# Five output banks, slot tables before the last gather evictions, tile-wise transfers, and memory products that wait for banks

## The reference, cut to what matters

```python
# per layer, x is (512, 1024), mem is (256, 1024)
x = x + mixers(rms_norm(x)) @ w_mix_out            # latent attention, pooling, window attention, convolution
kv = rms_norm(mem) @ xa_w_kv                       # (256, 512)
x = x + cross_attention(rms_norm(x) @ w_q, kv) @ w_o
t = rms_norm(x)
g = argmax(t @ w_group); top2 = top_k(softmax((t @ w_expert)[group g]), 2)
for e in range(32):                                # only for tokens that chose e
    y = (silu(t_e @ w_gate[e]) * (t_e @ w_up[e])) @ w_down[e]
    x[tokens of e] += weight * y
```

## Time and profile before

| | |
|---|---|
| Median of 3 runs | 1267.82 us (1262.52 to 1271.57) |
| The profiled execution | 1269.59 us, its span 1267.9 us |
| TensorE busy, mean granted clock | 1190.8 us (94%), 0.966 |
| VectorE / ScalarE / GpSimd busy | 696.0 / 326.3 / 46.4 us |
| Chain that ended last | PE 85%, DVE 7%, issue 2%, ACT 2%, DMA 1% |

### The profile page before, as it was taken

The page is one execution under the profiler, slowest core; times in us unless marked ns, Lnnn a source line. Parts: engine busy times, 40 slices in busy tenths (PEclk is TensorE's granted clock), DMA queues, the critical chain, the costliest instruction groups (busy, mean ns, idle before and its releaser), DMA issues.

```text
span 1267.9 us, 17480 instructions
## 1 busy us (share of the span) xinstructions
PE 1190.8 (94%) x5132; PEld 653.3 (52%) x5132; DVE 696.0 (55%) x1627; ACT 326.3 (26%) x731; POOL 46.4 (4%) x89
## 2 busy tenths in 40 slices
PE   6999999999698999999979999999996899999996
PEld 3754555556593444444457545555565744444443
DVE  3345564467674555555542365545767745555554
ACT  4215231024312222222142152211242222222221
POOL 7000000000006000000000000000000000000000
PEclk9999998999798999999989999989997999999999
DMA  9140023400405999999541300245004089999981
GB/s 284 33 132 1 1 67 123 177 34 1 199 1 179 401 422 422 422 422 422 201 143 32 102 1 1 67 133 199 1 2 199 1 316 404 421 422 422 422 374 67
DMA packets 52549, 243.14 MB, mean 192 GB/s; under 512 B 8320, under 2 KB 18848, under 8 KB 27392
## 3 DMA queue, kind: packets, MB, share of 16 engines
q1 hardware_dynamic: 49344, 240.40, 48.0%
q0 software_dynamic: 2560, 1.89, 0.9%
q10 hardware_dynamic: 576, 0.02, 0.0%
HBM read 240.19 MB, written 2.10 MB: 191 GB/s over the span
## 4 chain that ended last, share of the span: by engine, by line
PE 85%; DVE 7%; issue 2%; ACT 2%; DMA 1%; DVEq 1%; ACTq 1%; SPq 0%
PE ps L2519 18%; PE ps L2124 10%; PE ps L2552 9%; PE ps L2344 8%; PE ps L2116 7%; PE ps L2503 6%; PE ps L2504 4%; PE ps L2094 4%; PE ps L2145 4%; PE ps L2489 2%; PE ps L2392 2%; PE ps L2186 2%; PE ps L2488 2%; DMA X<-in_x 1%; PE ps L2194 1%
## 5 line engine op out<-in xcount | busy, mean ns | idle before, releaser
L2519 PE MATMUL ps<-wgu,xw 128*64 128x512 f32 x1024 | 228.8, 600 | 7.8 <-ACTq L1179 6.7
L1958 DVE TENSOR_TENSOR X<-ps,X 128x512 f32<-128x512 f32 x256 | 156.0, 682 | 10.9 <-issue 9.0
L2124 PE MATMUL ps<-hT,ring 128*128 128x512 f32 x352 | 158.4, 606 | 0.0
L2519 PEld LDWEIGHTS ps<-wgu,xw 128*64 128x64 f32 x1024 | 76.8, 138 | 153.9 <-issue 153.9
L2552 PE MATMUL ps<-wdn,hhT 128*64 128x512 f32 x512 | 120.3, 613 | 2.8 <-ACTq L1197 2.8
L2344 PE MATMUL ps<-ring,yT 128*128 128x512 f32 x256 | 119.5, 616 | 0.4 <-DVE X L1356 0.4
L2503 PE MATMUL ps<-yhi,Wt 128*128 128x512 f32 x256 | 114.1, 446 | 3.7 <-DVEq L1242 3.7
L2124 PEld LDWEIGHTS ps<-hT,ring 128*128 128x128 f32 x352 | 67.4, 196 | 78.2 <-issue 78.2
L2504 PE MATMUL ps<-ylo,Wt 128*128 128x512 f32 x256 | 101.1, 395 | 0.0
L1976 DVE SCALAR_TENSOR_TENSOR ylo<-ps,ws,yhi 128x512 fp32r<-128x512 f32 x64 | 48.1, 751 | 74.1 <-ACTq L1207 74.1
L1965 DVE TENSOR_TENSOR hh<-ps,silu 128x256 f32<-128x256 f32 x32 | 13.6, 425 | 124.6 <-ACTq L1185 124.6
(11 more groups left out here) (367 smaller groups left out, 1505.0 us busy)
## 6 DMA issues: line engine op xcount, KB each, us to landing
wgu<-in_w_gate SPq DMA_DIRECT2D x64, 1024.0 KB, 9.0
wgu<-in_w_up SPq DMA_DIRECT2D x64, 1024.0 KB, 11.1
wdn<-in_w_down SPq DMA_DIRECT2D x64, 1024.0 KB, 10.9
ring<-in_w_in SPq DMA_DIRECT2D x8, 1024.0 KB, 6.6
ring<-in_w_mix_out SPq DMA_DIRECT2D x12, 512.0 KB, 6.0
w_kv<-in_xa_w_kv SPq DMA_DIRECT2D x2, 2048.0 KB, 10.0
ring<-in_w_in SPq DMA_DIRECT2D x2, 2048.0 KB, 17.6
ring<-in_w_in SPq DMA_DIRECT2D x2, 1536.0 KB, 16.6
```

What stands on the lines that cost most here:

```text
L1958: tt(xh, bank, xh, ALU.add).then_inc(mfreed((what, n)), 1)
L2124: last = mm(bank, w[:, c, c0:c0 + P], hT[:, c, :], start=c == 0, stop=c == KD - 1)
L2519: last = mm(bank[r], xw[:, c, r], wgu[2 * parity + j][:, :, c, :], start=c == 0, stop=c == KD - 1)
```

## The change

- **Banks.** `comb` 0 to 4 go to banks 0, 1, 2, 3 and 5, `comb` 5 to 7 to banks 0 to 2; the last comb turns over all five. `hhT` goes to bank 4, the one of `gu`.
- **Tables.** `diag` and `ranked` lie in the down weights' last buffer, so that `placed` can run before `sorted_gain(1)`. TensorE makes `places` and `wslot` right behind the gather (`slots`), before step 0. Half of the first window is copied during the gather, the register for the other half is read ahead, and ACT copies `places` out before step 0's silu. SP sends pair 1's last down load only when `wslot` is done.
- **Transfers.** `memx`, `w_kv`, `X` and the output go in 2, 2, 4 and 4 pieces with semaphores of their own. DVE signals `gathered` first at the program's start, and `x_final` after every two additions of the last comb.
- **Start.** TensorE waits for the MoE jobs' last frees of all eight banks, not for `layer_done`. POOL loads `pos_i` after it has built `ident`.

```diff
@@ moe_plans
+    back_banks = (0, 1, 2, 3, 5)
             for n in range(5):
-                b.use(("comb", n), n % 4)
-        b.use(("hhT",), 5)
+                b.use(("comb", n), back_banks[n])
+        b.use(("hhT",), 4)
         if back:
             for n in range(5, 8):
-                b.use(("comb", n), n % 4)
+                b.use(("comb", n), back_banks[n - 5])
     for n in range(8):
-        tail.use(("last comb", n), n % 4)
+        tail.use(("last comb", n), back_banks[n % 5])
@@ SBUF
-        diag = at("diag", [P, 2 * NT, P], F32, late + 4096)
+        diag = at("diag", [P, 2 * NT, P], F32, 3 * E_BYTES + 16384)
+        ranked = at("ranked", [P, 2 * NT, P], F32, 3 * E_BYTES + 20480)
@@ sync
-                sp.dma_start(memx[:], mem_d).then_inc(mem_in, 16)
-                sp.dma_start(w_kv[:], cols("xa_w_kv", l, 0, 512)).then_inc(w_kv_in, 16)
+                for i in range(NM):
+                    sp.dma_start(memx[:, i], mem_d[:, i]).then_inc(mem_in[i], 16)
+                for part in range(2):
+                    c = slice(part * KD // 2, (part + 1) * KD // 2)
+                    sp.dma_start(w_kv[:, c], cols("xa_w_kv", l, 0, 512)[:, c]).then_inc(w_kv_in[part], 16)
                 with sp.If(l < 1):
-                    sp.dma_start(X[:], x_d).then_inc(x_in, 16)
+                    for t in range(NT):
+                        sp.dma_start(X[:, t], x_d[:, t]).then_inc(x_in[t], 16)
...
-                load_pair(l, 1, 1)
+                load_gate_up(l, 1, 1)
+                load_down(l, 1, 1, (0,))
+                multiplied(l, 0, ("wslot",))
+                load_down(l, 1, 1, (1,))
...
-            sp.wait_ge(S["layer_done"], DEPTH + 1)
-            sp.dma_start(out_d, X[:]).then_inc(x_out, 16)
-            sp.wait_ge(x_out, 16)
+            for t in range(NT):
+                sp.wait_ge(S["x_final"], done(DEPTH - 1, "x_final", t + 1))
+                sp.dma_start(out_d[:, t], X[:, t]).then_inc(x_out, 16)
+            sp.wait_ge(x_out, NT * 16)
@@ gpsimd
-            pool.dma_start(pos_i[:], pos_d, allow_slow_non_contiguous=True).then_inc(pos_in, 16)
             pool.memset(ident[:], 0.0)
...
             pool.nop().then_inc(ident_ready, 1)
+            pool.dma_start(pos_i[:], pos_d, allow_slow_non_contiguous=True).then_inc(pos_in, 16)
@@ scalar
+                wait_apart(act, S["starts_ready"], done(l, "starts_ready", 1))
+                second = act.value_load(starts[0:1, 1:2], min_val=0, max_val=2 * SEQ)
                 for half in range(HALVES):
+                    if half == 1:
+                        act.wait_ge(S["xgT_dve"], done(l, "xgT_dve", KD // 2))
+                        wait_apart(act, S["G_used"], done(l, "G_used", NT + 2))
+                        copy(xw[:, :, 0:SLOTS], xgT[:, :, 0:SLOTS])
...
-                wait_apart(act, S["starts_ready"], done(l, "starts_ready", 1))
                 wait_apart(act, S["xgT_dve"], done(l, "xgT_dve", KD))
-                windows(0)
+                copy(xw[:, :, SLOTS:2 * SLOTS], xgT[:, :, bass.ds(second, SLOTS)])
+                act.drain()
+                act.nop().then_inc(S["xw_ready"], 1)
+                for k in range(2):
+                    bank = mfull(act, l, 0, ("places", k))
+                    copy(places[:, k], bank).then_inc(mfreed(("places", k)), 1)
@@ vector
+                placed()
                 sorted_gain(1)
-                placed()
                 overflow_tiles()
...
-                bring_back(PAIRS - 1, "last comb", range(8))
+                for t in range(NT):
+                    bring_back(PAIRS - 1, "last comb", (2 * t, 2 * t + 1))
+                    signal("x_final")
@@ tensor
-                pe.wait_ge(S["layer_done"], l + 1)
+                for bank in range(8):
+                    back_in_layer = head.free[bank] + (PAIRS - 2) * step.free[bank] + tail.free[bank]
+                    pe.wait_ge(moe_free[bank], l * back_in_layer + 1)
...
+                slots()
                 step_(0, 0, False)
```

More of the change, by code:

```diff
@@ L460, in build @@
         hh = at("hh", [P, FF], F32, late + 5120)
+        all_ones = at("all_ones", [P, P], F32, late + 5120)
         over = at("over", [P, 2 * P], F32, late + 6144)
@@ L682, in load_gate_up, with load_down @@
                     sp.dma_start(flat[:, 1, :], expert(wu_d, e)).then_inc(gu_in[s], 16)
-            def load_down(l, pair_of_layer, ps_):
-                for j in range(2):
+            def load_down(l, pair_of_layer, ps_, which=(0, 1)):
+                for j in which:
                     s = 2 * ps_ + j
@@ L1186, in step_ @@
                     act.nop().then_inc(S["silu_ready"], 1)
-                    if isinstance(p, int) and p == 0:
-                        for k in range(2):
-                            bank = mfull(act, l, 0, ("places", k))
-                            copy(places[:, k], bank).then_inc(mfreed(("places", k)), 1)
-                            act.drain()
-                            act.nop().then_inc(S["places_ready"], 1)
                     if ahead:
@@ L1372, in is_first @@
                 dve.drain()
+            for s_ in (S["gathered"], S["layer_done"], S["route_ready"]):
+                dve.sem_inc(s_, 1)
             for bank in range(8):
@@ L1377, in _ @@
                 dve.sem_inc(moe_free[bank], 1)
-            for s_ in (S["layer_done"], S["gathered"], S["route_ready"]):
-                dve.sem_inc(s_, 1)
             for j in range(16):
@@ L2208, in _ @@
                         last.then_inc(filled(("memT", i, h)), 1)
-                pe.wait_ge(w_kv_in, (l + 1) * 16)
                 for i in range(NM):
                     pe.wait_ge(S["hmT_ready"], done(l, "hmT_ready", 2 * i + 2))
-                    tokens(l, ("kvx", i), hmT, i, w_kv, 0, 512)
+                    bank = bank_of(l, ("kvx", i))
+                    for c in range(KD):
+                        if c % 4 == 0:
+                            pe.wait_ge(w_kv_in[2 * c // KD], (l + 1) * 16)
+                        last = mm(bank, hmT[:, c, i * P:(i + 1) * P], w_kv[:, c, :], start=c == 0, stop=c == KD - 1)
+                    last.then_inc(filled(("kvx", i)), 1)
                 for t in range(NT):
@@ L2508, in uses_before, with slots @@
                     return l * (PAIRS // 2) + (p // 2 if isinstance(p, int) else i + (1 if parity == 0 else 0))
+                def slots():
+                    pe.wait_ge(S["place_ready"], done(l, "place_ready", 1))
+                    for k in range(2):
+                        bank = mbank_of(l, 0, ("places", k))
+                        mm(bank, all_ones[:], diag[:, NT * k:NT * (k + 1), :], start=True, stop=True
+                           ).then_inc(mfilled(("places", k)), 1)
+                    bank = mbank_of(l, 0, ("wslot",))
+                    for g in range(2 * NT):
+                        weighed = rt[:, 13 + g // NT, (g % NT) * NE:(g % NT + 1) * NE]
+                        last = mm(bank[:, 0:NE], ranked[:, g, :], weighed, start=g == 0, stop=g == 2 * NT - 1)
+                    last.then_inc(mfilled(("wslot",)), 1)
                 def step_(p, parity, back):
@@ L2525, in step_ @@
                         bring_back(p, "comb", range(5), 1 - parity)
-                    else:
-                        pe.wait_ge(S["place_ready"], done(l, "place_ready", 1))
-                        for k in range(2):
-                            bank = mbank_of(l, p, ("places", k))
-                            mm(bank, W1[:, 0:P], diag[:, NT * k:NT * (k + 1), :], start=True, stop=True
-                               ).then_inc(mfilled(("places", k)), 1)
-                        bank = mbank_of(l, p, ("wslot",))
-                        for g in range(2 * NT):
-                            weighed = rt[:, 13 + g // NT, (g % NT) * NE:(g % NT + 1) * NE]
-                            last = mm(bank[:, 0:NE], ranked[:, g, :], weighed, start=g == 0, stop=g == 2 * NT - 1)
-                        last.then_inc(mfilled(("wslot",)), 1)
                     pe.wait_ge(S["hh_ready"], mdone(l, p, "hh_ready", 1))
```

26 lines of the change are left out of this document (16 added, 10 removed).

## The result

The changed kernel takes 1249.97 us (median of 4 runs, 1245.98 to 1250.87), the kernel before, with one more run than above, 1269.1 (4 runs, 1262.52 to 1271.57). The ratio is 0.9852, with a 95% interval of 0.9827 to 0.9877. The profiled execution took 1250.87 us, its span 1249.1; that is 18.7 us under the profiled execution of before.

What follows compares the result with a forecast made beforehand. TensorE, busy 94% of the span, was taken as the bound, with the weights' stream nearly a second. The terms -10.5 - 7.0 + 1.5 + 0.3 - 3.1 = -18.8 us gave 1249 us from 1267.82; range 1241 to 1259.

Steps and rivals of the forecast that it cites:

- Term 1: Expert-pair steps: with five banks, comb 4, 6 and 7 stop waiting for additions; 30 x 0.35 = -10.5 us.
- the two signs that I had named for being wrong: Expert-pair steps: TensorE waits for gu_in in layer 1, or a step stays at 14.95 us.
- Term 2: Tables ahead and step 0: no pause before gu, down product starts earlier; -3.5 us per layer, -7.0 in all.
- Term 3: Program start: positions land later, so the w_kv products start 2.6 us later; +1.5 us at the transposes.
- Term 4: Between the layers: dropping the layer_done wait gains nothing, eight new waits cost perhaps +0.3 us.
- Term 5: Program end: three quarters of the output go out while the additions run; -3.1 us.
- The four with a name: Start gains after all (0.10), only half of step 0 comes (0.15), banks don't free TensorE (0.12), slower (0.03).
- the slow one: Program start: positions' load finds no turn until big loads are through at about 34 us; 1273 us; chance 0.03.
- The one of the weights' stream: Expert-pair steps: additions or weights' stream (14.91 us a step) set the pace, Term 1 near 0; 1259 us; chance 0.12.

Runs made afterwards that it cites:

- the one with the filler: TensorE makes 24 unread transposes of the identity ahead of the layer loop, added to the run that waits only for banks needed next; 1243.09 us, ratio 0.9802.
- the positions first: Changed kernel with GpSimd sending the positions' load ahead of the identity, as before the change; 1247.55 us, ratio 0.9827.

## Why the prediction came true, term by term

- **Term 1** (-10.5): right in mechanism and place. Measured -10.6: 30 steps of 0.37 are -11.1, and the weights took 0.5 back in layer 1. The slack that I put at 0.5 us was -0.5, an error of 1 us. So one of the two signs that I had named for being wrong did come: TensorE waited for `gu` weights in layer 1, in the last steps and for 0.5 us in all.
- **Term 2** (-7.0): measured -6.6. `gu` started 0.4 us later behind the gather than before in layer 1, and 0.6 in layer 2, not 0.25, and took 7.09 where 6.9 was forecast. Its working had the right parts, but I called the clock's share a matter of any pause; the run with the slot products in step 0 shows `gu` at the full level behind 2.58 us. I costed SyncE's wait for `wslot` at nothing. It does cost nothing where it stands, but that is held up by the slot products coming first: with them 11 us later, `gu` of step 1 to the last comb took 5.4 us more.
- **Term 3** (+1.5): measured +0.2 at the first `w_in` product, and -0.1 at the transposes that I had forecast (33.95 against 34.08). It was mis-sized in three pieces. I moved the identity up by the 0.9 us that the issue takes, where it moved by 3.05; GpSimd's idle time behind its own load was the piece I left out, so the positions went out at 2.37 and not 4.0, and although they took 6.9 us to land and not 6.0, `hmT` began at 14.20 and its products at 16.00 in place of 16.6. The w_kv products took 15.60 and not 16.9, because the level rose earlier, and that is luck: from the same start they took 15.9, 16.5 and 16.8 in three other runs. "5.2 to 6.5" for the small loads was read too narrowly (4.7 to 6.65 in that trace). The packets weren't all of 8 KB, as the sentence and the estimate have it: of the 748 packets over 2 KB that moved from 1 to 14 us in the changed kernel, 492 were under 8 KB. By the estimate from the rule that I quoted from the Trainium skill (DMA: Bandwidth & Descriptors, "Queues, rings and completion order"), 6 to 21 us to land, the trace agrees with the low end, and nothing here reaches the rest.
- **Term 4** (+0.3): measured +0.7, and the reason was wrong. I had the pause be TensorE's own way back and the new waits cost time. The waits show no cost, and what the pause consists of stays open (3.50 to 4.84 us with no wait in the way). The 0.7 goes to the drains of term 5, done in layer 1 too for nobody: last comb to first transpose takes 9.99 to 10.73 us in the four kernels with them and 8.78 to 9.70 in seven of the eight without, the eighth (10.12) being the one with the filler. What failed here is that I costed those drains at 0.25 us each and only at the end: they add 1.07 us to the additions, in both layers. As to the Trainium skill's rule (Runtime: NRT & Kernel Launch, "Instruction fetch mechanics") that a taken branch out of the fetched window waits for a fetch: 3.5 us or more do stay in every kernel, and no run here shows that it is the fetch.
- **Term 5** (-3.1): measured -2.9; with the drains' part between the layers it is worth -2.1.
- **The rivals.** The four with a name fell: the time is 1250, and each term came near its forecast. In the working of the slow one, the load that makes the program slower than before lands at 28.8 us, not at about 27: landing at 10.0 costs 1.5 us, and 20.3 are reached 18.8 us later. The one of the weights' stream was nearer than its chance of 0.12 says: with `wslot` 11 us later, and the loads behind it held up by 5, it was true in layer 1.
- **The sum** was exact partly by luck: the terms measured come to -19.2, the start 1.3 under its forecast and terms 2, 4 and 5 together 1.0 over theirs, and +0.3 lies in no term. What is in no term can be far larger: the attention part of layer 1, the same code, took 338.4 to 345.2 us in the profiles.

## What to carry to other kernels

When a stall is taken out of a loop whose loads already run at the full rate, work out how many steps the slack lasts, and look at every wait that stands ahead of those loads in the queue: the same gain can be there or gone by one transfer that is sent 11 us later and holds the next ones up by 5 us. A drain can cost more than its own time where scalar reads or a branch follow, and a semaphore that is incremented anyway (a bank's release) may carry the same message for nothing. A pause that gets shorter is no gain if the work before it got longer: measure it from a fixed start. Effects of 1 to 3 us are read from stretches cut at fixed places in the trace, not from whole times, as long as the clock moves a stretch by 1.7 us from one execution to the next.

## What the runs showed of the hardware

- GpSimd's step behind a drain begins only when a load that it issued itself has landed: 4.12 landed and 4.44 begun before, 7.48 and 7.80 with the positions first, 9.31 and 9.54 in the changed kernel. With no load of its own ahead the same step begins 0.3 us after the one before it.
- The first products behind a pause can run at half speed (the lower of the two levels, 1.2 GHz and not 2.4) for a time that changes from one execution to the next. In four kernels with the same start the w_kv products begin at 16.0 us, and the transposes behind them at 31.44, 31.76, 32.36 and 32.72. In the changed kernel the granted clock in the windows reads 1.00 there, although a product takes 1061 ns and later 592; in two of the others (the slot products back, the output in one piece) it reads 0.5. So in this place it is the products' durations that tell the level.
- A pause of 1.6 us ahead of the w_kv products was followed by no slow product in one run and by three in another, and one of 3.0 us by seven; ahead of step 0's `gu` none followed 2.6 us, in two cases.
